# Attention heads placed between projection chunks, one sum of squares per half, and a reordered gate and merge stage, in a two-layer decoder trunk

## The chip, the cores and the metric

One Trainium2 chip, all 8 NeuronCores. Each core runs the same program on 2 of the 16 sequences, with no exchange between cores. The metric is the device time of one execution, in microseconds (us), taken on the slowest core.

## The reference, cut to what matters

The trunk has two layers. Width is 1024, the sequence 2048, the memory 256 tokens, with 4 heads of 256 in the cross-attention and 2816 hidden channels in the MLP.

```python
for l in range(DEPTH):                                    # DEPTH = 2
    h = rms_norm(x, mix_norm_g[l])
    proj = h @ w_in[l]
    a, gl, u_pool, g_conv, g_pool = jnp.split(proj, split_at, axis=-1)
    yc = a * sigmoid(gl)                                  # GLU, 512 channels
    yc = causal_dwconv(yc, conv_dw_w[l]) + conv_dw_b[l]   # 31 taps
    yc = silu(layer_norm(yc, conv_ln_g[l], conv_ln_b[l])) @ w_conv_out[l]
    zp = multiscale_pool(u_pool)
    yp = einsum("bsgc,gcd->bsgd", zp, w_pool_grp[l]).reshape(b, s, d) * pool_scale[l]
    merged = sigmoid(g_conv) * yc + sigmoid(g_pool) * yp
    x = x + merged @ w_out[l]
    hq = rms_norm(x, xattn_norm_g[l])                     # cross-attention into mem
    q = hq @ w_q[l];  k, v = split(mem_n @ w_kv[l])
    x = x + (softmax(q k^T / 16) v) @ w_o[l]              # 4 heads
    hf = rms_norm(x, ffn_norm_g[l])
    gate, val = split(causal_dwconv(hf @ w_up[l], ffn_dw_w[l]))
    x = x + (gelu(gate) * val) @ w_down[l]
return rms_norm(x, final_norm_g)
```

## The kernel before, in words

**Tiling.** Each core takes 2 sequences in 2 parts of T = 1024 positions (`hf` 0 and 1): 4 units, each through 2 layers, so **8 passes** of mixer, attention and MLP. Channels lie on the 128 partitions and positions on the free axis. The residual stream `X` is 8 tiles of 128x1024 float32, its normed copy `H` 8 tiles in bf16. Positions are worked in two halves of 512 (`s` = 0 and 1, `ST` = 512), because a matmul writes one PSUM bank of 128x512 float32. A *chunk* is 128 output channels of one half: 8 matmuls of 128x512 over the 8 input tiles (11 in the down projection) into one bank. An evacuation then reads the bank.

**What sets the order.** `Sched` keeps one list of instructions per engine, in the order in which the Python code adds them, and puts a semaphore wait where a tile written elsewhere is read, or a tile still in use is overwritten. There is no reordering: what is written first on an engine runs first there, and what stands behind a waiting instruction waits too. PSUM banks come from `Banks`, a rotation of 8: `P.next()` takes the bank used longest ago, so a chunk cannot start until that bank has been read. `P.take()` removes a bank from the rotation, and `P.release` appends it again. `defer(fn, lag)` puts work off until `lag` chunks later (`tick()` counts them).

**Weights** come in blocks of 1 MB through a ring of 5 slots (`ring_get`), issued on POOL. Copies between SBUF tiles and loads and stores of x are issued on SP.

**Mixer** (`mixer`). First `a` and `gl` are projected, half by half. `glu` takes the sigmoid of `gl` on ACT, and one DVE instruction multiplies the bank of `a` with it and writes the product in bf16 in *phase order* (position 4n+j goes to j*256+n), at line 763. After half 1, `to_phases` copies the product by DMA into the 16 convolution tiles `CV`. The convolution is 16 groups of 9 matmuls with 128x256, with the pooling branch, three up chunks and the first gate half-chunks between them. `stats_mm` sums for the LayerNorm. `ln_finish` computes mean and reciprocal deviation, then for each quarter q two DVE instructions on 128x1024 (line 865: subtract, multiply), four SILU activations of 128x256 and their copies by DMA (line 872). Then `gate_half` is called for the next gates. A gate k (0 to 15) is two half-chunks q = 2k and 2k+1, each with a sigmoid from its bank into a tile `GB`. There are 8 such tiles, so gate 8 needs the tile of gate 0, which the merge must have read. Before the merge, gates 0 to 7 are done. The merge goes over 8 output tiles i: for each half 5 matmuls from the silu and pooling results with the weights `WX`, and three DVE instructions (line 943, one at line 411, one at line 401) into `MG[i]`. Two gates follow i = 0, and one gate follows each of i = 1 to 6. In the last layer before a new sequence, and once at the start, the norm of the memory (`mem_squares`, `mem_finish`) lies in the same place.

**Output projections** (`residual_stage`) take the input tiles `MG`, the attention result `ATT`, or the MLP's hidden tiles. Two banks are taken for the sums of squares. All 8 chunks of half 0 come first (the first three, or two, as a *lead group* with the input tile as the outer loop), then the 8 of half 1. The evacuation of chunk `oc` is: DVE adds the bank to `X`, ACT squares, and DVE adds the square to the running sum of its group of four chunks:

```python
if oc % 4:
    TT("dve", sq.v(), sq.v(), prev_sq[s].v(), ALU.add)
prev_sq[s] = sq
if oc % 4 == 3:
    defer(lambda: MM(pn[s].v(), ONESK.v(), sq.v(), oc == 3, oc == 7), 3, tag)
```

So there are two matmuls with the ones matrix `ONESK` per half, three chunks after oc = 3 and after oc = 7. After the second come Ln and Exp on ACT (`norm_stats_fin`) and 8 instructions on DVE that write `H` (`norm_apply`, line 411), two per chunk. The half-0 ones stand between the evacuations of half 1.

**Attention** (`attn`). All 16 query chunks come first, half 0 and then half 1. Then for each head and half: 4 matmuls for the scores, 2 Exp on ACT, 2 matmuls with ones (the denominator), Ln and Exp on ACT, 4 matmuls with the values, 2 multiplications on DVE into `ATT`. The names in the trace are `AR,KV` for scores and values and `AR,ONES` for the denominator. Then the output projection.

**MLP** (`ffn`). It is not changed, apart from its down projection's use of `residual_stage`. In the last layer that stage also carries the final norm, the stores of the result, and the norm of the next unit's first input (`unit_norm`).

In the profile most instructions carry the line of a helper: L424 is every matmul, L397 every activation, L401 `tensor_tensor`, L411 `scalar_tensor_tensor`. `AR` is the arena in which most tiles lie. Tile names there tell operations apart.

## Time and profile before

| what | us |
|---|---|
| median of 3 runs | 4116.72 |
| lowest and highest | 4114.6, 4533.86 |
| the profiled execution | 4116.1 |
| its span, slowest core (core 6) | 4114.6 |
| spans of the 8 cores | 4102.6 to 4114.6 |
| PE busy | 3876.9 (94%) |
| DVE busy | 2683.5 (65%) |
| ACT busy | 1953.7 (47%) |

The profiled execution's time lies 1.5 us over its span and 0.6 us under the median, so terms worked out inside the span can be taken off the median as they are. The 8 passes lie one behind the other in the span, each a little over 500 us long. A busy PE is not PE at its peak: matmuls are pipelined, and their ends are modelled. What a stretch of matmuls lost is found by comparing its start-to-start time with the number of matmuls in it.

### The profile page before, as it was taken

The numbers are of one execution on the slowest core, as the hardware profiler recorded it, in microseconds if no ns is written. First come the engines' busy times: TensorE is split into PE (matmuls) and PEld (weight loads), VectorE is DVE, ScalarE is ACT, GpSimd is POOL, SyncE is SP. The second block draws the span as 40 slices with busy tenths as digits, with TensorE's granted clock in tenths as the row PEclk, the third lists the DMA queues.
The fourth block names the chain that finished last, engine by engine and source line by source line (L and its number), as shares of the span: only waits on it lengthen the run. The fifth ranks groups of instructions, "written<-read, shape, count | busy, mean of one in ns | idle before, by whom it ended". The sixth has DMA issues, their size and how long they took to land.

```text
span 4114.6 us, 56669 instructions; the slowest of 8 cores (4102.6 to 4114.6 us)
## 1 busy us (share of the span) xinstructions
PE 3876.9 (94%) x18224; PEld 1784.1 (43%) x18224; DVE 2683.5 (65%) x3336; ACT 1953.7 (47%) x3779; POOL 197.7 (5%) x379
## 2 busy tenths in 40 slices
PE   6999999999998999999989999999999999999998
PEld 3444444444443445434444444543444434444343
DVE  4538775387754876649675387653867549665587
ACT  3445444464444544446443464434644346452544
POOL 1000000000000000000010000000000000000000
PEclk9999999999999999999999999999999999999999
DMA  6443352434842345323464424534346424352342
GB/s 138 117 82 68 65 107 58 82 68 80 168 103 51 59 78 110 62 49 67 106 136 103 84 56 81 99 64 84 65 108 136 103 49 73 68 106 52 57 75 70
DMA packets 108815, 348.19 MB, mean 85 GB/s; under 512 B 11888, under 2 KB 46960, under 8 KB 83952
## 3 DMA queue, kind: packets, MB, share of 16 engines
q0 software_dynamic: 41760, 275.11, 37.0%
q1 hardware_dynamic: 66768, 69.46, 5.7%
q8 instruction: 155, 2.54, 0.3%
q14 instruction: 132, 1.08, 0.1%
HBM read 586.05 MB, written 16.78 MB: 147 GB/s over the span
## 4 chain that ended last, share of the span: by engine, by line
PE 81%; ACT 7%; DVE 6%; issue 3%; DMA 2%; SPq 0%; DVEq 0%; ACTq 0%; POOLq 0%; POOL 0%
PE ps L424 81%; DVE X L401 2%; ACT SQ L397 2%; DVE H L411 2%; ACT F L397 2%; ACT AR L397 2%; DMA AR<-AR 1%; DVE SQ L401 1%; DVE X L411 1%; ACT RS L397 0%; DMA AR<-xT 0%; SPq L872 0%; ACT L397 0%; DVE F L411 0%; DMA RING<-wst 0%
## 5 line engine op out<-in xcount | busy, mean ns | idle before, releaser
L424 PE MATMUL ps<-H,RING 128*128 128x512 bf16 x10240 | 2265.0, 381 | 66.4 <-ACT GB L397 25.3
L424 PEld LDWEIGHTS ps<-H,RING 128*128 128x128 bf16 x10240 | 1004.2, 98 | 1286.6 <-issue 110.7
L424 PE MATMUL ps<-AR,RING 128*128 128x512 bf16 x4864 | 1096.7, 386 | 0.0
L397 ACT ACTIVATE AR<-ps 128x512 bf16<-128x512 f32 (+1 forms) x1024 | 598.5, 600 | 637.8 <-PE ps L424 610.8
L411 DVE SCALAR_TENSOR_TENSOR F<-AR,VEC,F 128x1024 f32<-128x1024 bf16 (+1 forms) x576 | 687.9, 1194 | 111.8 <-ACT F L397 69.1
L424 PEld LDWEIGHTS ps<-AR,RING 128*128 128x128 bf16 x4864 | 482.7, 99 | 590.2 <-issue 39.1
L397 ACT ACTIVATE SQ<-X 128x512 bf16<-128x512 f32 x384 | 240.2, 629 | 599.8 <-DVE X L401 561.9
L401 DVE TENSOR_TENSOR X<-ps,X 128x512 f32<-128x512 f32 x512 | 339.6, 684 | 200.3 <-PE ps L424 200.2
L397 ACT ACTIVATE GB<-ps 128x512 bf16<-128x512 f32 x320 | 183.1, 604 | 433.1 <-PE ps L424 431.5
L397 ACT ACTIVATE GB<-F 128x1024 bf16<-128x1024 f32 x192 | 189.3, 986 | 287.0 <-DVE F L411 286.4
L515 POOL DMA_DIRECT2D RING<-wst x280 | 147.8, 528 | 3598.7 <-PE ps L424 3578.4
L401 DVE TENSOR_TENSOR SQ<-SQ 128x512 bf16<-128x512 bf16 x288 | 122.5, 425 | 258.6 <-ACT SQ L397 249.7
L401 DVE TENSOR_TENSOR AR<-ps,F 128x512 bf16<-128x512 f32 x128 | 82.4, 686 | 318.9 <-PE ps L424 305.0
L411 DVE SCALAR_TENSOR_TENSOR H<-X,VEC,RS 128x512 bf16<-128x512 f32 x320 | 222.3, 749 | 86.5 <-ACT RS L397 86.5
L397 ACT ACTIVATE F<-ps,VEC 128x512 f32<-128x512 f32 x352 | 242.9, 690 | 0.0
L411 DVE SCALAR_TENSOR_TENSOR GB<-AR,VEC,F 128x1024 bf16<-128x1024 bf16 x192 | 229.4, 1195 | 20.4 <-DVE F L411 0.5
L943 DVE TENSOR_TENSOR F<-ps,GB 128x512 f32<-128x512 f32 x128 | 88.0, 687 | 160.8 <-PE ps L424 160.7
L763 DVE TENSOR_TENSOR AR<-ps,GB 128x512 bf16<-128x512 f32 x64 | 154.9, 2446 | 34.9 <-ACT GB L397 21.5
L424 PE MATMUL ps<-AR,WX 128*128 128x512 bf16 x640 | 149.9, 379 | 3.8 <-DMA AR<-AR 3.4
L401 DVE TENSOR_TENSOR AR<-GB 128x1024 bf16<-128x1024 bf16 x192 | 124.3, 648 | 20.8 <-ACT F L397 0.9
L406 DVE TENSOR_SCALAR F<-AR,VEC 128x1024 f32<-128x1024 bf16 x192 | 135.0, 703 | 1.2 <-ACT AR L397 0.2
L424 PE MATMUL ps<-AR,KV 128*128 128x512 bf16 x512 | 122.1, 378 | 0.0
(75 smaller groups left out, 1954.5 us busy)
## 6 DMA issues: line engine op xcount, KB each, us to landing
RING<-wst POOLq DMA_DIRECT2D x184, 1024.0 KB, 9.3
RING<-wst POOLq DMA_DIRECT2D x64, 704.0 KB, 7.8
RING<-wst POOLq DMA_DIRECT2D x32, 768.0 KB, 6.7
AR<-AR SPq DMA_DIRECT2D x256, 64.0 KB, 3.5
X<-xT SPq DMA_DIRECT2D x64, 256.0 KB, 12.8
yT<-X SPq DMA_DIRECT2D x64, 256.0 KB, 9.4
AR<-xT SPq DMA_DIRECT2D x40, 256.0 KB, 7.0
WX<-wst POOLq DMA_DIRECT2D x8, 1280.0 KB, 15.9
```

The costliest lines, as they stand in the source:

```text
L397: S.add("act", lambda h: h.activation(out=out.ap, in_=in_.ap, func=func, scale=s, **kw), reads=rd, writes=out.keys)
L401: S.add(eng, lambda h: h.tensor_tensor(out=out.ap, in0=a.ap, in1=b.ap, op=op), reads=a.keys + b.keys, writes=out.keys)
L406: S.add(eng, lambda h: h.tensor_scalar(out=out.ap, in0=a.ap, scalar1=s, scalar2=None, op0=op0), reads=a.keys + k, writes=out.keys)
L411: S.add(eng, lambda h: h.scalar_tensor_tensor(out=out.ap, in0=a.ap, scalar=s, in1=b.ap, op0=op0, op1=op1), reads=a.keys + b.keys + k, writ ...
L424: S.add("pe", lambda h: h.matmul(out.ap, lhsT=lhsT.ap, rhs=rhs.ap, start=start, stop=stop), reads=lhsT.keys + rhs.keys, writes=out.keys)
L515: S.add("pool", lambda h, d=dst, s_=src: h.dma_start(out=d, in_=s_), reads=after, writes=RING[slot].v().keys, dma_sem="ring%d" % slot)
L763: S.add("dve", lambda h: h.tensor_tensor(out=o_ap, in0=a_ap, in1=g_ap, op=ALU.mult), reads=psa[c].v().keys + sub(sgs[c], s).keys, writes=G ...
L943: S.add("dve", lambda h, p_ap=p_ap, g_ap=g_ap, o_ap=o_ap: h.tensor_tensor(out=o_ap, in0=p_ap, in1=g_ap, op=ALU.mult), reads=psc.v().keys + ...
```

## The change

- **Sums of squares.** The running sum goes over all 8 chunks of a half and is added one chunk late: at chunk oc >= 2 DVE adds the squares of oc-2 and before to that of oc-1. At oc = 7 there is one more add. One matmul with `ONESK` per half is left, three chunks after oc = 7.
- **Attention.** Scores and heads of half 0 stand between the query chunks of half 1, and those of half 1 between the output chunks of half 0. `run_items` is the chunk loop taken out of `proj_group`.
- **Gates.** Half-gates 6 to 9 are computed inside `ln_finish`, one behind each quarter's four silus, and evacuated there as plain copies (Copy) to the float32 tiles F0 and F1. Their sigmoids are taken from there after gate 6. Gates 8, 9 and 10 get tiles of their own (`SQ`, `TW[0]`) and are computed before the merge. In the merge one gate follows each of i = 0 to 4.
- **LayerNorm.** The subtraction of quarter 1 stands before the multiplication of quarter 0.
- **GLU.** The multiplication walks its elements in another order: the output runs contiguously, and the two inputs are read with a step of 4 elements.

```diff
-            prev_sq = {}
+            sqs = [[], []]
...
                     ACT(sq.v(), sub(X[oc], s), AF.Square)
-                    if oc % 4:
-                        TT("dve", sq.v(), sq.v(), prev_sq[s].v(), ALU.add)
-                    prev_sq[s] = sq
+                    sqs[s].append(sq)
+
+                    def add():
+                        a, b_ = sqs[s].pop(0), sqs[s][0]
+                        TT("dve", b_.v(), b_.v(), a.v(), ALU.add)
+
+                    if oc >= 2:
+                        add()
                     tag = 2 if last else s
-                    if oc % 4 == 3:
-                        defer(lambda: MM(pn[s].v(), ONESK.v(), sq.v(), oc == 3, oc == 7), 3, tag)
                     if oc == 7:
+                        add()
+                        defer(lambda: MM(pn[s].v(), ONESK.v(), sq.v(), True, True), 3, tag)
...
-                    o_ap = GLU[c].ap.rearrange("p (j n) -> p n j", j=4)[:, s * 128:(s + 1) * 128, :]
-                    a_ap = psa[c].ap.rearrange("p (n j) -> p n j", j=4)
-                    g_ap = sub(sgs[c], s).ap.rearrange("p (n j) -> p n j", j=4)
+                    o_ap = GLU[c].ap.rearrange("p (j n) -> p j n", j=4)[:, :, s * 128:(s + 1) * 128]
+                    a_ap = psa[c].ap.rearrange("p (n j) -> p j n", j=4)
+                    g_ap = sub(sgs[c], s).ap.rearrange("p (n j) -> p j n", j=4)
...
+                for q in range(4):
+                    if q != 1:
+                        ln_op(q, mu, ALU.subtract)
+                    if q == 0:
+                        ln_op(1, mu, ALU.subtract)
+                    ln_op(q, va, ALU.mult)
                     for r in range(4):
...
-            def gate_half(q):
+                    gate_half(6 + q, GP[q])
+                    done.add(6 + q)
+
+            GP = [F[0].v(0, ST), F[0].v(ST, T), F[1].v(0, ST), F[1].v(ST, T)]
...
-                ACT(sub(gates[k], s), ps.v(), AF.Sigmoid)
+                if park is None:
+                    ACT(gates[k][s], ps.v(), AF.Sigmoid)
+                else:
+                    ACT(park, ps.v(), AF.Copy)
+                    parked.append((gates[k][s], park))
...
-            for k in range(3, 8):
+            for k in range(3, 11):
                 do_gate(k)
-                if has_mem and k == 6:
-                    mem_squares()
+                if k == 6:
+                    for o_, i_ in parked:
+                        ACT(o_, i_, AF.Sigmoid)
+                    if has_mem:
+                        mem_squares()
...
-                for _ in range(2 if i == 0 else 1):
-                    if k_next < 16:
-                        do_gate(k_next)
-                        k_next += 1
+                if k_next < 16:
+                    do_gate(k_next)
+                    k_next += 1
...
+            flush_tag((0,))
+            run_items(qi, 0)
+            flush()
+            for hd in range(3):
+                scores(hd, 0)
+                if hd == 0:
+                    lead_group(qi[0:4], 1)
+                else:
+                    run_items(qi[2 * hd + 2:2 * hd + 4], 1)
+                heads(hd, 0)
+            scores(3, 0)
+            scores(0, 1)
+            heads(3, 0)
+            heads(0, 1)
             wab = [ring_get(l, "woa0"), ring_get(l, "woa1")]
-            residual_stage([(wab[oc // 4], 512, (oc % 4) * 128, ATT) for oc in range(8)], "H", LB + 72, 3)
+            oi = residual_items([(wab[oc // 4], 512, (oc % 4) * 128, ATT) for oc in range(8)], "H", LB + 72)
+            for hd in range(1, 4):
+                scores(hd, 1)
+                run_items(oi[2 * hd - 2:2 * hd], 0)
+                heads(hd, 1)
+            run_items(oi[6:8], 0)
+            run_items(oi, 1)
```

The order of the instructions moves at three places. First PE, from the last matmuls of the LayerNorm sums (`SQ,MASK`) through the merge (`AR,WX`) into the output projection (`AR,RING`) of the first pass, before:

```order
L424 MATMUL ps<-SQ,MASK 128x512 x2
L424 MATMUL ps<-H,RING 128x512 x80
L424 MATMUL ps<-MEMN,ONESK 128x256 x8
L424 MATMUL ps<-AR,WX 128x512 x10
L424 MATMUL ps<-H,RING 128x512 x32
L424 MATMUL ps<-AR,WX 128x512 x10
L424 MATMUL ps<-H,RING 128x512 x16
L424 MATMUL ps<-AR,WX 128x512 x10
```

And the same place in the changed kernel; the last three rows are the end of the merge:

```order
L424 MATMUL ps<-SQ,MASK 128x512 x2
L424 MATMUL ps<-H,RING 128x512 x128
L424 MATMUL ps<-MEMN,ONESK 128x256 x8
L424 MATMUL ps<-AR,WX 128x512 x10
L424 MATMUL ps<-H,RING 128x512 x16
L424 MATMUL ps<-AR,WX 128x512 x10
...
L424 MATMUL ps<-H,RING 128x512 x16
L424 MATMUL ps<-AR,WX 128x512 x30
L424 MATMUL ps<-AR,RING 128x512 x80
```

48 matmuls of three gates moved ahead of the merge, and its last 30 matmuls (i = 5, 6 and 7) now stand together, with no gate between them and the output projection.

Second ACT, at the same place: the Ln and Exp of the LayerNorm (`RS<-RS`), the silus (`AR<-AR,VEC`) and the gates, before:

```order
L397 ACTIVATE RS<-RS 128x256
L397 ACTIVATE AR<-AR,VEC 128x256 x16
L397 ACTIVATE GB<-ps 128x512 x8
L397 ACTIVATE MEMN<-F 128x256 x8
L397 ACTIVATE GB<-ps 128x512 x2
```

And in the changed kernel:

```order
L397 ACTIVATE RS<-RS 128x256
L397 ACTIVATE AR<-AR,VEC 128x256 x4
L397 ACTIVATE F<-ps 128x512
L397 ACTIVATE AR<-AR,VEC 128x256 x4
L397 ACTIVATE F<-ps 128x512
L397 ACTIVATE AR<-AR,VEC 128x256 x4
L397 ACTIVATE F<-ps 128x512
L397 ACTIVATE AR<-AR,VEC 128x256 x4
L397 ACTIVATE F<-ps 128x512
L397 ACTIVATE GB<-ps 128x512 x4
L397 ACTIVATE GB<-F 128x512 x4
L397 ACTIVATE MEMN<-F 128x256 x8
```

The four copies `F<-ps` free four banks between the silus, and the four sigmoids `GB<-F` are new work behind them.

Third PE in the attention, from the queries (`H,RING`) into the output projection, before:

```order
L424 MATMUL ps<-H,RING 128x512 x128
L424 MATMUL ps<-AR,KV 128x512 x4
L424 MATMUL ps<-AR,ONES 128x512 x2
L424 MATMUL ps<-AR,KV 128x512 x8
L424 MATMUL ps<-AR,ONES 128x512 x2
...
L424 MATMUL ps<-AR,KV 128x512 x4
L424 MATMUL ps<-AR,RING 128x512 x48
L424 MATMUL ps<-SQ,ONESK 128x512
L424 MATMUL ps<-AR,RING 128x512 x32
L424 MATMUL ps<-SQ,ONESK 128x512
```

And in the changed kernel, the first head and then the place where the halves meet:

```order
L424 MATMUL ps<-H,RING 128x512 x64
L424 MATMUL ps<-AR,KV 128x512 x4
L424 MATMUL ps<-H,RING 128x512 x32
L424 MATMUL ps<-AR,ONES 128x512 x2
...
L424 MATMUL ps<-AR,ONES 128x512 x2
L424 MATMUL ps<-AR,KV 128x512 x12
L424 MATMUL ps<-AR,ONES 128x512 x2
L424 MATMUL ps<-AR,KV 128x512 x4
L424 MATMUL ps<-AR,ONES 128x512 x2
L424 MATMUL ps<-AR,KV 128x512 x8
L424 MATMUL ps<-AR,RING 128x512 x16
```

Between the scores of a head and its matmuls with ones there are now 16 or 32 matmuls of a projection, or, in the middle, 4 of another head.

## Rows read from the trace of the kernel before

**Rows 1.** Page, part 1: busy us, share of the span, instructions

```profile
PE 3876.9 (94%) x18224; PEld 1784.1 (43%) x18224; DVE 2683.5 (65%) x3336; ACT 1953.7 (47%) x3779; POOL 197.7 (5%) x379
```

**Rows 2.** Waits of PE: releaser, us in total, times, longest us

```profile
PE ps L424 <- DVE SQ L401: 85.0, 48, 4.3
PE ps L424 <- ACT AR L397: 31.6, 65, 0.5
```

**Rows 3.** Timeline of PE in the attention: start, us, work, [idle before <-releaser]

```profile
1779.13 1.03 PE L424 MATMUL ps<-AR,KV 128*128 128x512 bf16 x4
...
1786.73 0.76 PE L424 MATMUL ps<-AR,ONES 128*128 128x512 bf16 x2 [0.51 <-ACT AR L397]
...
1789.72 0.76 PE L424 MATMUL ps<-AR,ONES 128*128 128x512 bf16 x2 [0.51 <-ACT AR L397]
```

**Rows 4.** Timeline of PE in the attention's output projection

```profile
1803.17 10.52 PE L424 MATMUL ps<-AR,RING 128*128 128x512 bf16 x48
...
1831.64 0.59 PE L424 MATMUL ps<-SQ,ONESK 128*128 128x512 bf16 x1 [2.52 <-DVE SQ L401]
...
1836.83 3.62 PE L424 MATMUL ps<-H,RING 128*128 128x512 bf16 x16
```

**Rows 5.** Timeline of DVE in that projection, half 1

```profile
1824.92 1.42 DVE L411 SCALAR_TENSOR_TENSOR H<-X,VEC,RS 128x512 bf16<-128x512 f32 x2 [0.87 <-ACT RS L397]
...
1827.83 0.42 DVE L401 TENSOR_TENSOR SQ<-SQ 128x512 bf16<-128x512 bf16 x1 [0.89 <-ACT SQ L397]
1828.17 1.41 DVE L411 SCALAR_TENSOR_TENSOR H<-X,VEC,RS 128x512 bf16<-128x512 f32 x2
```

**Rows 6.** Timeline of PE, gates before the merge, and the merge

```profile
1646.61 13.98 PE L424 MATMUL ps<-H,RING 128*128 128x512 bf16 x64
1664.07 5.29 PE L424 MATMUL ps<-H,RING 128*128 128x512 bf16 x16 [3.48 <-ACT GB L397]
...
1687.67 3.62 PE L424 MATMUL ps<-H,RING 128*128 128x512 bf16 x16
1691.12 2.32 PE L424 MATMUL ps<-AR,WX 128*128 128x512 bf16 x10
```

**Rows 7.** Windows: us, busy us (x) of PE, PEld, DVE, ACT, POOL; PEclk; DMA share, GB/s

```profile
1664.00:1673.00 9.00, 8.65 (x35) 3.71 (x36) 0.23 (x1) 8.42 (x19) 0.53 (x1) 0.81 0.35 71
```

**Rows 8.** Timeline of ACT at the silus

```profile
1653.34 8.19 ACT L397 ACTIVATE AR<-AR,VEC 128x256 bf16<-128x256 f32 x16
1661.54 1.28 ACT L397 ACT_TABLE_LOAD   x1
1662.84 4.03 ACT L397 ACTIVATE GB<-ps 128x512 bf16<-128x512 f32 x8
```

**Rows 9.** Timeline of DVE in the merge

```profile
1692.26 0.69 DVE L943 TENSOR_TENSOR F<-ps,GB 128x512 f32<-128x512 f32 x1 [1.41 <-PE ps L424]
...
1694.32 0.68 DVE L943 TENSOR_TENSOR F<-ps,GB 128x512 f32<-128x512 f32 x1
```

**Rows 10.** Timeline of PE in the mixer's output projection

```profile
1715.73 10.52 PE L424 MATMUL ps<-AR,RING 128*128 128x512 bf16 x48
...
1745.63 0.38 PE L424 MATMUL ps<-SQ,ONESK 128*128 128x512 bf16 x1 [3.95 <-DVE SQ L401]
...
1750.98 3.62 PE L424 MATMUL ps<-H,RING 128*128 128x512 bf16 x16
```

**Rows 11.** Timeline of DVE in that projection, half 1, its first norm instructions

```profile
1738.90 1.41 DVE L411 SCALAR_TENSOR_TENSOR H<-X,VEC,RS 128x512 bf16<-128x512 f32 x2 [2.30 <-ACT RS L397]
```

**Rows 12.** Timeline of PE where a new unit begins

```profile
2109.71 3.40 PE L424 MATMUL ps<-H,RING 128*128 128x512 bf16 x15 [3.35 <-DVE AR L763]
2118.48 2.08 PE L424 MATMUL ps<-AR,GB 128*128 128x256 bf16 x9 [5.38 <-DMA AR<-AR]
```

**Rows 13.** Lines 763 and 943: count, ns min/median/max, first and last start

```profile
L763 DVE TENSOR_TENSOR AR<-ps,GB x64: 2410/2432/2683, 49.3 to 3641.0; 128x512 bf16<-128x512 f32 x64
L943 DVE TENSOR_TENSOR F<-ps,GB x128: 680/685/693, 149.0 to 3747.8; 128x512 f32<-128x512 f32 x128
```

More of the change, by code:

```diff
@@ L649, in proj_group, with run_items @@
                     lead_group(items[:lead[s]], s)
[L650 to L657 removed]
+                run_items(items[lead[s]:], s)
+        def run_items(items, s):
+            for blk, ncol, col0, rhs, evac in items:
+                b_ = blk(s) if callable(blk) else blk
+                nk = len(rhs)
+                ps = P.next()
+                for kc in range(nk):
+                    MM(ps.v(), b_.v(kc * ncol + col0, kc * ncol + col0 + 128), sub(rhs[kc], s), kc == 0, kc == nk - 1)
+                evac(s, ps)
+                tick()
         def norm_stats_fin(s, pn):
@@ L859, in ln_finish, with ln_op @@
                 P.release(pst)
-                for q in range(4):
+                def ln_op(q, vv, op):
                     y = YCQ[q]
                     y_ap = y.ap.rearrange("p (g n) -> p g n", g=4)
-                    for vv, op in ((mu, ALU.subtract), (va, ALU.mult)):
-                        v_ap = vv.ap.unsqueeze(1).to_broadcast([128, 4, 256])
-                        S.add("dve", lambda h, v_ap=v_ap, y_ap=y_ap, op=op: h.tensor_tensor(out=y_ap, in0=y_ap, in1=v_ap, op=op),
-                              reads=y.v().keys + vv.keys, writes=y.v().keys)
+                    v_ap = vv.ap.unsqueeze(1).to_broadcast([128, 4, 256])
+                    S.add("dve", lambda h: h.tensor_tensor(out=y_ap, in0=y_ap, in1=v_ap, op=op),
+                          reads=y.v().keys + vv.keys, writes=y.v().keys)
+                for q in range(4):
[4 more added lines that the diff above has]
+                    ln_op(q, va, ALU.mult)
                     for r in range(4):
@@ L881, in gate_half @@
                 if s == 0:
-                    gates[k] = GBR.next()
+                    if k in (8, 9):
+                        gates[k] = [SQB[2 * k - 16].v(), SQB[2 * k - 15].v()]
+                    else:
+                        gb = TW[0] if k == 10 else GBR.next()
+                        gates[k] = [sub(gb, 0), sub(gb, 1)]
                 col = half * 256 + ii * 128
@@ L1003, in attn, with scores @@
-            wab = [ring_get(l, "woa0"), ring_get(l, "woa1")]
-            residual_stage([(wab[oc // 4], 512, (oc % 4) * 128, ATT) for oc in range(8)], "H", LB + 72, 3)
+            qi = [(wqb[qc // 4], 512, (qc % 4) * 128, H,
+                   (lambda s, ps, qc=qc: ACT(sub(Q[qc], s), ps.v(), AF.Identity, scale=1.0 / 16))) for qc in range(8)]
+            expd = {}
+            def scores(hd, s):
+                expd[hd, s] = []
+                for mc in range(2):
+                    ps = P.next()
+                    for dc in range(2):
+                        MM(ps.v(), KT[2 * hd + dc].v(mc * 128, (mc + 1) * 128), sub(Q[2 * hd + dc], s), dc == 0, dc == 1)
+                    e = EBR.next()
+                    ACT(e.v(), ps.v(), AF.Exp)
+                    expd[hd, s].append(e)
@@ new lines, in heads @@
+            def heads(hd, s):
+                E = expd.pop((hd, s))
+                psd = P.next()
+                for mc in range(2):
+                    MM(psd.v(), ONES1.v(), E[mc].v(), mc == 0, mc == 1)
+                rd = F[(2 * hd + s) % 4]
+                ACT(rd.v(0, ST), psd.v(), AF.Ln)
+                ACT(rd.v(0, ST), rd.v(0, ST), AF.Exp, scale=-1.0)
+                for dc in range(2):
+                    pso = P.next()
+                    for mc in range(2):
+                        MM(pso.v(), VV[mc].v(hd * 256 + dc * 128, hd * 256 + (dc + 1) * 128), E[mc].v(), mc == 0, mc == 1)
+                    TT("dve", sub(ATT[2 * hd + dc], s), pso.v(), rd.v(0, ST), ALU.mult)
```

50 lines of the change are left out of this document (11 added, 39 removed).

## The prediction

> **What bounds the kernel now.** I read the page's busy times first. PE is busy for 94% of the span, DVE for 65% and ACT for 47% [rows 1], so only what PE waits for counts. The second view is PE's waits by releaser: the longest sum belongs to the matmuls with `ONESK`, 85.0 us in 48 waits for DVE's running sum of squares, and 31.6 us go to the attention's exponentials [rows 2]. The third is PE's timeline, because those sums miss what a wait leaves behind. I compare each stretch's length with its matmuls: 16 of 128x512 take 1691.12 - 1687.67 = 3.45 us when nothing disturbs them, so 0.2157 us each [rows 6]. Whatever a stretch takes above that is lost. All terms are of one pass near the middle of the span and are multiplied by 8. They come off the profiled execution's 4116.1 us, which is the median (4116.72) within 0.6 us.
>
> **Heads between projection chunks.** From the first scores (1779.13) to the first matmul of the output projection (1803.17) lie 24.0 us [rows 3, 4] for 80 matmuls, worth 17.3 us: 6.8 us lost. The rows show how: one head and half takes 1789.72 - 1786.73 = 2.99 us for 10 matmuls (2.16 us), because PE has nothing to do between the scores and the matmuls with ones. Now 16 or 32 projection matmuls (3.5 or 6.9 us) lie there. ACT does 4 activations of about 0.6 us per head plus 2 evacuations, 3.6 us, while PE does 26 matmuls, 5.6 us, so ACT stays ahead. In the middle only 4 matmuls of another head (0.86 us) cover two Exp (1.1 us): I leave 0.8 us there. Gain 6.0 a pass, 48 us. Bounds: 0 (ACT's queue holds the projection's banks for as long) and 54.
>
> **Attention's output projection, with one sum per half.** It takes 1836.83 - 1803.17 = 33.7 us [rows 4] for 131 matmuls (28.3 us): 5.4 us lost, 2.52 of it in one wait. DVE is in order there: add into X, wait for ACT's square (0.89), add the square, and in half 1 two norm instructions: 3.25 us per chunk [rows 5], where PE needs 1.73. With the add one chunk late the 0.89 goes, 2.36 us are left. The early sum (oc = 3), on which PE stood, is gone with its two matmuls (0.43 us). What is late next is the last sum. Count from the start of half 1: the sum of half 0 can go after two chunks (3.5); then come DVE's add, the square, Ln and Exp, about 2.8, so the norm instructions start at 6.3; four periods of 2.36 end at 15.8; two more chunks, a square and the last add take 2.8: 18.6. PE, with 8 chunks, a sum and the next stage's two chunks behind it, is there at 17.5. So about 1.0 us is left. Gain 5.4 + 0.4 - 1.0 = 4.8 a pass, 38 us. Bounds: 0.4 (the wait only moves) and 5.8.
>
> **Gates between the silus.** PE does 64 gate matmuls and then stands 3.48 us for a bank [rows 6], because ACT is in 16 silus (8.19 us) and a table load (1.28) and empties none [rows 8]. The 16 matmuls behind it take 5.29 us instead of 3.62, in a stretch whose mean granted clock is 0.81, so partly at 1.2 GHz instead of 2.4 [rows 6, 7]. Together 5.15 us. A copy after each four silus (2.05 us) now frees a bank every 2.6 us or so. Half-gate 14, the first to reuse a bank, comes 8 x 1.73 = 13.8 us after half-gate 6, long after the first copy. The four copies and the four late sigmoids cost ACT 8 x 0.5 to 0.6 us, in a stretch that is now 48 matmuls (10.4 us) longer. These also cover the silus' transfers, for which the merge sometimes waited. Gain 5.0 a pass, 40 us. Bounds: 5.2 above; below, see the table rival.
>
> By the Trainium skill (ScalarE: Activation LUTs, section on table sets) cheap functions such as copy are in every set, so these copies need no load. No row here shows a Copy behind a silu.
>
> **The end of the merge pays for the gates.** DVE takes 1694.32 - 1692.26 = 2.06 us per tile and half [rows 9], PE 5 matmuls, 1.08 us. A gate (3.45 us) behind each tile hid this. Tiles 5, 6 and 7 now have none. DVE starts 1692.26 - 1691.12 = 1.14 us after PE [rows 6, 9]. The output projection opens with three chunks side by side, and by the rotation the third needs the bank that DVE reads at the fifth of these six steps: 1.14 + 4 x 2.06 + 0.69 = 10.1 us, and a signal. PE has finished its 30 matmuls at 6.5 and can do 2 more: 3.3 us idle, and as after the 3.48 us above some matmuls at the lower clock, 1.3. So +4.6 a pass. Bounds 0 and 5.5. Queued behind: the whole projection.
>
> **Mixer's output projection.** 1750.98 - 1715.73 = 35.3 us [rows 10] for the same 131 matmuls: 7.0 us lost, 3.95 in one wait. It differs from the attention's by a table load before Ln: DVE waits 2.30 us there instead of 0.87 [rows 11, 5]. That load stays, so by the count above the last sum is ready 1.4 us later, at 20.0 against PE's 17.5: 2.4 us, and 0.6 for the clock. So 7.0 + 0.4 - 3.0 = 4.4 gained, and 4.6 paid to the merge: -0.2 a pass, -2 us. This is where most of an expected gain should vanish.
>
> **Down projection.** Of the 85.0 us of waits for the sum, 8.5 a pass (1.0 + 3.95 and 1.0 + 2.5) are in the other two stages, which leaves 17. Its chunks are 11 matmuls (2.37 us), as long as DVE's new 2.36, so nearly all goes: 14 us.
>
> **GLU.** It takes 2432 ns for 512 elements, with writes 512 bytes apart. The merge's multiplication reads its bank 512 bytes apart and writes contiguously in 685 ns [rows 13]. So I take 0.69 us for the new form, whose reads step by 4 elements. Bounds: 0.68, and 4.9 (each of the two stepped reads as slow as the stepped write). In most passes no PE wait hangs on it. Where a new unit begins (3 times) PE stands 3.35 us for a bank that GLU holds and 5.38 for the transfer issued behind it [rows 12]; the other two show less of the second. I take 3.35, 1.4 of clock and 1.5 of the transfer, since the DMA queue is full there: 6.3 x 3 = 19 us.
>
> The Trainium skill has a rule against this part: by Advanced Engine Details and Errata, section Memory Cachelines, PSUM has lines of 8 bytes, and pairs of elements should be contiguous; it speaks of matmuls. The new read steps 16 bytes. By that rule GLU would stay slow, which is the third rival. The row of line 943 (685 ns) speaks against it, and the slow writes (2432 ns) fit its rule for SBUF.
>
> **Sum.** 48 + 38 + 40 - 2 + 14 + 19 = 157 us. 4116.7 - 157 = **3960 us**.
>
> **Rivals.**
> 1. *The queues of ACT and DVE bound the mixed stages.* The ATT multiplications, adds and squares now share an in-order queue with evacuations, so PE waits for banks in the middle of chunks. For it: DVE's period in half 1 exceeds PE's chunk already [rows 5]. Against it: ACT is 47% busy. Half of the heads' and the projection's gain goes: 3960 + 24 + 19 = 4003.
> 2. *Copy is not in silu's table set*: 8 loads of 1.28 us [rows 8] a pass, 10.3 us on ACT. The gates' 5 us is lost and another 5.3 spent at the merge's start: 3960 + 82 = 4042.
> 3. *GLU's stepped reads cost what the stepped writes did*: only the units' starts are lost, 3960 + 19 = 3979.
> 4. *The other side: both stepped reads are slow*, 4.9 us. The a/gl stage (27.6 us of matmuls) holds 8 x 2.4 = 19.5 us of GLU already, and with the norm and tap instructions DVE has little room, so 8 x 2.45 = 19.6 us a pass end up on PE: 3960 + 157 + 19 = 4136, slower than before. It decides from 2.43 + (157 - 19)/64 = 4.6 us. Line 943's row speaks against it.
>
> **How the numbers follow.** Forecast 0.68; rivals 1 to 4: 0.18, 0.03, 0.07, 0.04. Low end: if the new waits (0.8, 1.0, 4.6 and 3.0 a pass) were about 60% smaller, 45 us less, 3915. High end: rival 1 with 17 us more, 4020; beyond lie rivals 2 and 4 and a tail. A measurement of this kernel can tell about 2% (82 us) from no change; 4034 is that border. Faster by over 2%: 0.92; within 2%: 0.07 (rivals 2 and 4, the tail of 1); slower by over 2%: 0.01.
>
> **What would show it.** Right: PE's waits for `AR,ONES` near 5 us instead of 34; waits for the sum of squares near 25 us, all at the last sum of a half; no wait of PE for ACT's `GB` tiles behind the silus; a new gap of some 3 us between the last `AR,WX` and the first `AR,RING`, released by DVE; GLU at 0.69 us. Wrong: table loads between the silus; GLU above 2 us; matmul groups in the attention far over 0.2157 us each. If the merge's gap is missing, the time comes out near 3925.

## The result and the profile after

The changed kernel ran in 3961.56, 3947.66 and 3949.14 us. The ratio to the kernel before is **0.9604, interval 0.956 to 0.9649**: 4.0% faster, where 3960 us (0.962) was forecast. Most kernels also had executions some ten to some hundred microseconds longer, in which the cores of one die showed a lower clock; the ratios and times given here are of the other executions. Where two chips are compared I add the *middle core*: the median core span of the die that was the faster one in a run, and of these the median over all runs (before: 4111 us on the first experiments' chip, 4124 on the second, 4114 on the third; changed kernel: 3929).

That the total fits does not mean that its parts do. So I read the profile after in the same order as the one of before. The page gives the execution (core 2, the slowest) and its busy times:

```profile
span 3960.0 us, 56824 instructions; the slowest of 8 cores (3921.7 to 3960.0 us)
PE 3809.3 (96%) x18176; PEld 1776.8 (45%) x18176; DVE 2580.8 (65%) x3384; ACT 1955.8 (49%) x3811; POOL 206.6 (5%) x379
```

PE's matmuls went from 18224 to 18176: the 48 early sums of squares. DVE's busy time fell by 103 us and ACT's stayed as it was [rows 1]; ACT's share rose from 47% to 49% only because the span is shorter. PE's waits by releaser (us in total, times, longest us):

```profile
PE ps L424 <- DMA AR<-AR: 33.8, 6, 12.5
PE ps L424 <- DVE SQ L401: 27.8, 17, 2.5
PE ps L424 <- DVE F L976: 21.8, 18, 1.5
```

Three things are to be seen. The sum of squares has 27.8 us left of 85.0, and the attention's exponentials, 31.6 us before, are not in the list [rows 2]. DVE's `F L976` is new: it is the merge's multiplication, line 943 before. And the longest is now a transfer, `AR<-AR`, the copies of the GLU's product into the convolution's tiles. It was forecast to shrink. In the profile of before it read

```profile
PE ps L424 <- DMA AR<-AR: 12.6, 7, 5.4
```

**The merge's end** (PE's timeline; start, us, work, [idle before <-releaser]):

```profile
1170.33 6.64 PE L424 MATMUL ps<-AR,WX 128*128 128x512 bf16 x30
1178.47 0.38 PE L424 MATMUL ps<-AR,RING 128*128 128x512 bf16 x1 [1.50 <-DVE F L976]
1179.13 0.38 PE L424 MATMUL ps<-AR,RING 128*128 128x512 bf16 x1 [0.28 <-DVE F L411]
1180.52 1.87 PE L424 MATMUL ps<-AR,RING 128*128 128x512 bf16 x4 [1.02 <-DVE F L976]
...
1211.12 0.38 PE L424 MATMUL ps<-H,RING 128*128 128x512 bf16 x1 [0.15 <-DVE H L411]
1211.78 2.10 PE L424 MATMUL ps<-H,RING 128*128 128x512 bf16 x9 [0.29 <-DVE H L411]
1215.62 0.38 PE L424 MATMUL ps<-SQ,ONESK 128*128 128x512 bf16 x1 [1.74 <-DVE SQ L401]
```

From 1170.33 to 1180.52 are 10.19 us for 32 matmuls (6.90): 3.29 us lost, the new gap. The three rows behind it are the end of the mixer's output projection: 10 matmuls (2.16) between 1211.12 and 1215.62, so 2.3 us lost to norm instructions and the last sum of squares, 2.6 with the stretch just before. In the attention the middle, where the cover was thinnest, and the end of its output projection read:

```profile
1249.94 2.12 PE L424 MATMUL ps<-AR,KV 128*128 128x512 bf16 x8
1252.06 3.61 PE L424 MATMUL ps<-AR,RING 128*128 128x512 bf16 x16
...
1285.51 3.62 PE L424 MATMUL ps<-H,RING 128*128 128x512 bf16 x16
1290.19 0.38 PE L424 MATMUL ps<-SQ,ONESK 128*128 128x512 bf16 x1 [1.06 <-DVE SQ L401]
```

8 matmuls (1.73 us) take 2.12: 0.4 us is lost there, the same in all eight passes, and nowhere else among the heads. The last sum costs 1.2 us (4.68 for 16 matmuls).

**ACT at the silus** has one evacuation behind each four, and a table load at either end only:

```profile
1118.09 1.28 ACT L397 ACT_TABLE_LOAD   x1 [1.47 <-DVE AR L875]
1119.38 2.08 ACT L397 ACTIVATE AR<-AR,VEC 128x256 bf16<-128x256 f32 x4
1121.37 0.57 ACT L397 ACTIVATE F<-ps 128x512 f32<-128x512 f32 x1
...
1129.30 1.28 ACT L397 ACT_TABLE_LOAD   x1
```

**DVE.** The GLU's 64 instructions (ns min/median/max), and from DVE's timeline the first norm instructions in the mixer's output projection:

```profile
L773 DVE TENSOR_TENSOR AR<-ps,GB x64: 679/691/693, 49.6 to 3502.3; 128x512 bf16<-128x512 f32 x64
```

```profile
1203.45 1.41 DVE L411 SCALAR_TENSOR_TENSOR H<-X,VEC,RS 128x512 bf16<-128x512 f32 x2 [3.55 <-ACT RS L397]
...
1205.71 1.41 DVE L411 SCALAR_TENSOR_TENSOR H<-X,VEC,RS 128x512 bf16<-128x512 f32 x2
```

GLU fell from 2432 to 691 ns. DVE's period in half 1 is 1205.71 - 1203.45 = 2.26 us.

**Where a unit begins**, PE's timeline and the queue of SP on the same core; below it SP's queue of before, at the same place:

```profile
1030.70 27.79 PE L424 MATMUL ps<-H,RING 128*128 128x512 bf16 x128
1070.99 2.08 PE L424 MATMUL ps<-AR,GB 128*128 128x256 bf16 x9 [12.50 <-DMA AR<-AR]
```

```profile
1023.22 27.86 SPq L674 DMA_DIRECT2D yT<-X  x14
1051.22 3.33 SPq L758 DMA_DIRECT2D AR<-AR  x4
1054.64 7.54 SPq L674 DMA_DIRECT2D yT<-X  x2
1062.27 11.84 SPq L758 DMA_DIRECT2D AR<-AR  x12
```

```profile
1066.60 31.42 SPq L671 DMA_DIRECT2D yT<-X  x14
1099.00 3.26 SPq L748 DMA_DIRECT2D AR<-AR  x4
1102.35 1.01 SPq L671 DMA_DIRECT2D yT<-X  x2
1103.79 8.38 SPq L748 DMA_DIRECT2D AR<-AR  x8
```

The wait for the GLU's bank is gone and the 128 matmuls of `a` and `gl` run through in 27.8 us. But the transfer is waited for 12.50 us instead of the 5.38 and less of before [rows 12]. The windows say why (us; busy of PE, PEld, DVE, ACT, POOL; PEclk; DMA share; GB/s), of after and then of before:

```profile
1020.00:1070.00 50.00, 38.28 (x175) 16.87 (x174) 33.20 (x52) 15.51 (x26) 5.27 (x8) 0.91 1.02 192
```

```profile
1060.00:1110.00 50.00, 42.47 (x183) 17.81 (x181) 44.98 (x53) 16.79 (x28) 4.54 (x7) 0.97 0.98 190
```

The core's 16 DMA engines are busy throughout in both kernels, moving 190 GB/s: stores of the old unit, loads of the new one's x, weights. The copies stand behind 14 and 2 stores of 256 KB in SP's queue: the 14th store lands at 1070.5 us, the first copy at 1070.7. In PE's timeline of before, the convolution starts at this place with

```profile
1111.57 2.08 PE L424 MATMUL ps<-AR,GB 128*128 128x256 bf16 x9 [2.63 <-DMA AR<-AR]
```

The wait is now 9.9 us longer, for two reasons. PE comes to the convolution 35.3 us after the first store, where it was 42.3 (3.4 of these 7 us are the bank wait that is gone). And the copies are there 47.8 us after the first store, where it was 45.0 us. From issue to landing the stores take, by the page's median,

```profile
yT<-X SPq DMA_DIRECT2D x64, 256.0 KB, 19.4
```

and 9.4 before. The wait differs between cores and sets their spans. PE's sums for `AR<-AR` on cores 0 to 7 are 19.5, 2.4, 33.8, 21.6, 23.5, 13.2, 27.1 and 9.2 us (mean 18.8; before 7.4 to 12.8, mean 10.1), and the spans of the two cores that wait least and most are 3921.7 us (core 1) and 3960.0 us (core 2).

**Stage by stage.** I took the start of the first matmul of each stage in both timelines (the convolution's, the merge's, the first scores, the MLP's) and subtracted the lengths, over 8 passes. From the convolution to the end of the attention, 141.0 us went; forecast for that block, without the attention's last sum, which falls behind its border, 124 + 8 = 132. From the MLP to the next convolution, with the down projection and the start of the next unit, 12.5 us went; forecast 33 - 8 = 25. Ahead of the first convolution 1.1 went. The block in which the heads and gates lie gave 9 more than forecast, the block with the transfers gave half. In that block the three stretches that end at a new unit's convolution, called *the three starts* below, took 837.9 us on the slowest core before and 833.8 after: 4 us gained there. On the mean of the eight cores it was 837.2 and 821.7, so 15.5.

### The profile page after: what moved, and what is told of

Read it like the earlier page. It is cut to its first block, busy times and chain, and to the rows that moved or that the text cites. A ratio compares the mean times of both kernels' runs of the same rounds, so it can differ in the third digit from the quotient of the medians.

```text
span 3960.0 us, 56824 instructions; the slowest of 8 cores (3921.7 to 3960.0 us)
## 1 busy us (share of the span) xinstructions
PE 3809.3 (96%) x18176; PEld 1776.8 (45%) x18176; DVE 2580.8 (65%) x3384; ACT 1955.8 (49%) x3811; POOL 206.6 (5%) x379
## 4 chain that ended last, share of the span: by engine, by line
PE 89%; DVE 4%; DMA 3%; issue 2%; ACT 2%; SPq 1%; DVEq 0%; ACTq 0%; POOLq 0%; POOL 0%
PE ps L424 89%; DMA AR<-AR 2%; DVE X L401 1%; DVE F L411 1%; DVE F L976 1%; DVE SQ L401 1%; ACT AR L397 1%; DVE H L411 0%; DMA AR<-xT 0%; ACT F L397 0%; SPq L674 0%; DVE X L411 0%; DMA RING<-wst 0%; ACT SQ L397 0%; SPq L889 0%
## 5 line engine op out<-in xcount | busy, mean ns | idle before, releaser
L424 PE MATMUL ps<-AR,RING 128*128 128x512 bf16 x4864 | 1074.7, 381 | 22.5 <-DVE F L976 20.2
L397 ACT ACTIVATE AR<-ps 128x512 bf16<-128x512 f32 (+1 forms) x1040 | 607.6, 600 | 633.2 <-PE ps L424 606.1
L397 ACT ACTIVATE GB<-F 128x1024 bf16<-128x1024 f32 (+1 forms) x224 | 206.9, 938 | 288.9 <-DVE F L411 288.1
L397 ACT ACTIVATE GB<-ps 128x512 bf16<-128x512 f32 x240 | 139.1, 599 | 337.0 <-PE ps L424 335.5
L401 DVE TENSOR_TENSOR SQ<-SQ 128x512 bf16<-128x512 bf16 x336 | 140.3, 418 | 30.1 <-ACT SQ L397 25.9
L976 DVE TENSOR_TENSOR F<-ps,GB 128x512 f32<-128x512 f32 x96 | 65.8, 686 | 134.8 <-PE ps L424 134.8
L397 ACT ACTIVATE SQ<-ps,VEC 128x256 bf16<-128x256 f32 x256 | 107.5, 472 | 49.0 <-PE ps L424 45.4
```

The lines of the kernel that those rows point to most:

```text
L397: S.add("act", lambda h: h.activation(out=out.ap, in_=in_.ap, func=func, scale=s, **kw), reads=rd, writes=out.keys)
L401: S.add(eng, lambda h: h.tensor_tensor(out=out.ap, in0=a.ap, in1=b.ap, op=op), reads=a.keys + b.keys, writes=out.keys)
L424: S.add("pe", lambda h: h.matmul(out.ap, lhsT=lhsT.ap, rhs=rhs.ap, start=start, stop=stop), reads=lhsT.keys + rhs.keys, writes=out.keys)
L976: S.add("dve", lambda h, p_ap=p_ap, g_ap=g_ap, o_ap=o_ap: h.tensor_tensor(out=o_ap, in0=p_ap, in1=g_ap, op=ALU.mult), reads=psc.v().keys + ...
```

## The experiments

Four kernels ran on each of three chips, each kernel beside runs of the kernel before on its own chip. Differences against the changed kernel are differences of ratios times 4117 us. The changed kernel's own interval is 0.9%, so each of them is uncertain by about 20 us; what the profile of a run shows at the place in question is therefore read beside it: the waits, and the lengths of these same stages, mean of the eight cores. Each kernel has one profiled execution.

### Is the unit's start bound by the transfers?

**e1: the GLU in its old element order** (writes 512 bytes apart), the rest as changed.

```diff
-o_ap = GLU[c].ap.rearrange("p (j n) -> p j n", j=4)[:, :, s * 128:(s + 1) * 128]
-a_ap = psa[c].ap.rearrange("p (n j) -> p j n", j=4)
+o_ap = GLU[c].ap.rearrange("p (j n) -> p n j", j=4)[:, s * 128:(s + 1) * 128, :]
+a_ap = psa[c].ap.rearrange("p (j n) -> p n j", j=4)
```

(and the same for the sigmoid's tile)

> The changed kernel with the GLU multiplication in its old element order (2.43 us instead of 0.69), all else kept. Theory A (the transfers bound the start of a unit): the first convolution group waits there for 4 MB of stores of the result that were issued ahead of its copies, so a slower GLU changes only who is waited for: within 5 us of the changed kernel's 3955. Theory B (my forecast's step): the faster GLU is worth 19 us at the three starts of a unit, so about 3974. Both: the five other passes show no difference.

**e2: the changed kernel, the 16 stores of a finished unit issued behind the 16 copies.** `norm_apply` only keeps them, and the mixer issues them after its `flush_all()`:

```diff
+                if (b, hf) == units[-1]:
+                    store()
+                else:
+                    pend_out.append(store)
...
                 flush_all()
+                while pend_out:
+                    pend_out.pop(0)()
```

> The changed kernel with the 16 stores of a unit's result issued on SP behind the 16 copies into the convolution tiles, at the three places where another unit follows. Theory A (the copies stand behind the stores in SP's queue and in the DMA engines): PE's waits for AR<-AR, 33.8 us in the profile, fall to under 5, and with the lower clock after them some 30 to 37 us go: 3918 to 3925. Theory B (the DMA engines are full anyway, with weights and the next input, so order does not matter): the waits stay above 25 us and the time stays within 8 us of 3955.

Measured: e1 0.963 (0.9608 to 0.9652), so 11 us slower than the changed kernel (23 by the middle core, 3952 for 3929); e2 0.9548 (0.953 to 0.9566), 23 us faster than it, where 30 to 37 were expected. The two ran on one chip, and the 34 us between them have an interval of 12 either way. PE's waits of e1 and of e2 (slowest core each):

```profile
PE ps L424 <- DMA AR<-AR: 25.6, 8, 9.7
PE ps L424 <- DVE AR L773: 10.1, 3, 3.4
```

```profile
PE ps L424 <- DMA AR<-AR: 1.3, 2, 0.8
```

In e1 the bank wait of before is back, 3.4 us at each of three starts, and so is a long transfer wait, mean 16.7 us over the cores. The long transfer wait is not the new GLU's doing: it is there without it. What the GLU is worth here the times leave open, 11 or 23 us; the three starts took 833.9 us for the changed kernel's 821.7, so 12.2. In e2 the transfer wait is gone, on every core at most 4.5 us, the spans lie within 3921.4 to 3936.9, and the three starts took 803.3 us. e2's windows and PE's timeline:

```profile
1020.00:1070.00 50.00, 49.49 (x233) 22.48 (x232) 38.51 (x61) 22.19 (x37) 5.30 (x9) 1.00 0.78 143
```

```profile
1038.93 27.79 PE L424 MATMUL ps<-H,RING 128*128 128x512 bf16 x128
1066.55 1.15 PE L424 MATMUL ps<-AR,GB 128*128 128x256 bf16 x9
```

The convolution follows without a gap, and the clock stays up. The stores issued ahead of the copies were the cause. Whether they hold the copies back by their place in the queue or by the load that they put on the DMA engines is not separated: e2 changes both, and in its window the share is 0.78 instead of 1.02. The Trainium skill (DMA: Bandwidth & Descriptors, section on queues, rings and completion order) says that descriptors on one DMA engine are consumed in ring order; the trace agrees as far as it goes, since the first copy lands just behind the 14 stores issued ahead of it.

**e8 and e9: the same two edits on the kernel before**, the new GLU order alone, and the late stores alone.

> The kernel before with the new element order of the GLU multiplication alone. Theory A (the start of a unit is bound by the DMA engines): the waits of PE for DVE AR L763 (10.1 us in three) go and its waits for AR<-AR there grow by nearly as much; 4110 to 4117. Theory B (the forecast's term): 19 us less, 4098. In the five other passes nothing changes although DVE is 14 us a pass less busy.

> The kernel before with the 16 stores of a unit's result issued behind the copies into the convolution tiles. Theory A (the same backlog was there before the change, hidden in part by PE's own delays): PE's waits for AR<-AR, 7.4 to 12.8 us by core, fall to the 2 or 3 us of the merge, but the 3.35 us waits for the GLU's bank stay: 8 to 12 us less, ratio 0.997. Rival (the change itself made the backlog, before it there was none to speak of): ratio 1.000.

Measured: e8 0.991 (0.9886 to 0.9934), 37 us with an interval of 10 either way, more than either theory gave; e9 0.9948 (0.9928 to 0.9968), 21 us, double what was expected. Both are likely too large: on these two chips one die's clock was 0.972 to 0.984 in the runs of before, where the first chip has 0.986. By the middle cores (median of the runs) e8 gains 36 us and e9 12; by the lowest of them, which are least touched by the clock, e8 gains 4107.2 - 4084.3 = 23 us and e9 4108.8 - 4099.9 = 9. The three starts, 837.2 us before, took 819.1 in e8 and 833.2 in e9: 18.1 and 4.0 less. In e8 the bank wait is gone and so is most of the transfer wait (at most 5.4 us by core, 7.4 to 12.8 before):

```profile
PE ps L424 <- DMA AR<-AR: 2.2, 3, 1.1
```

The copies are issued when half 1's GLU has run; a GLU that is 1.7 us shorter lets them start sooner, and the bank wait and the transfer wait both fall: 10.1 + 7.6 us on the mean core. So on the kernel before, the forecast's 19 us were there. In the changed kernel the starts show 12.2 of them (e1). That the other edits ate the rest, by bringing PE to a queue that was still full, is argued and not shown: e4 below does not touch the starts, and its 814.6 us for 821.7 says how far two profiled executions differ there.

**e10: both, late stores with the old GLU**, to see whether the GLU counts when the transfers no longer bind.

> Stores behind the copies, as in the second experiment, with the GLU's old element order. Theory A (once the transfers no longer bound the start of a unit, the GLU's time shows): 3 x 3.35 us for the bank, the clock behind it and the later copies: 12 to 20 us more than the second experiment's 3936, so 3948 to 3956. Theory B (GLU was worth the 10 us of the first experiment for other reasons, equal in both): 3946 with no wait of PE for DVE AR.

Measured 0.9558 (0.9515 to 0.96), against e2's 0.9548 on another chip. The bank wait is back:

```profile
PE ps L424 <- DVE AR L778: 10.1, 3, 3.4
PE ps L424 <- DMA AR<-AR: 2.6, 3, 1.1
```

The ratios do not settle it, since their intervals overlap; the middle cores do: 3943 against e2's 3923, and 3 of these 20 us lie between the chips. The three starts took 820.6 us, for e2's 803.3. With the transfers out of the way the GLU is worth some 17 us, near the 19.

### The parts of the gain

**e4: the attention in its old order**, all 16 query chunks, then head after head, then the output projection; one sum per half is kept. `heads` and `scores` are written back as one loop over `hd` and `s`, with `proj_group` ahead of it and `residual_stage` behind.

> The changed kernel with the attention in its old order (all queries, then all heads one behind the other, then the output projection), the one sum per half kept. Theory A (the heads' own waits are what the interleaving takes away, and nothing else): 8 x 6.4 = 51 us more, 4006, with PE's waits for AR,ONES back at 34 us and the output projection as in the changed kernel. Rival: the output projection also gained from the heads between its chunks (its first half has slack on DVE), then 60 us or more.

**e5: the old sums of squares**, the rest as changed.

```diff
-                    sqs[s].append(sq)
...
-                    if oc >= 2:
-                        add()
+                    if oc % 4:
+                        TT("dve", sq.v(), sq.v(), prev_sq[s].v(), ALU.add)
+                    prev_sq[s] = sq
+                    if oc % 4 == 3:
+                        defer(lambda: MM(pn[s].v(), ONESK.v(), sq.v(), oc == 3, oc == 7), 3, tag)
```

> The changed kernel with the old running sums: one sum per four chunks, added at once, two matmuls with ONESK per half. Theory A (the prediction's terms): mixer's projection 7.0 - 2.6 + 0.4 = 4.8 us a pass, attention's 5.4 - 1.2 + 0.4 - 1.0 (its first half now has slack between the heads) = 3.6, down projection 2.0: 10.4 x 8 = 83 us, 4038. Rival (the sums cost only what PE waited for them, 85 - 28 = 57 us, and the waits at the lower clock nothing): 4012. PE's waits for DVE SQ should be 70 to 85 us.

Measured: e4 0.973 (0.9703 to 0.9756), 52 us back for 48 forecast; e5 0.979 (0.9771 to 0.9809), 77 us back. The waits of e4, and of e5:

```profile
PE ps L424 <- ACT AR L397: 31.8, 65, 0.5
PE ps L424 <- DVE SQ L401: 27.9, 17, 2.5
```

```profile
PE ps L424 <- DVE SQ L401: 83.5, 44, 4.3
```

Each edit brings back its own wait, and not the other's. The two do not lean on each other: neither rival, in which the sums took what the heads gave, or the other way, holds. The middle cores agree for e4 (3977, 48 more than 3929), and for e5 (4022, 93 more, 80 if the chips' 13 us come off). From the convolution to the MLP e4 took 51.7 us more. In the forecast the sums had 38 + 14 and, in the mixer, (7.0 + 0.4 - 3.0) x 8 = 35: 87 in all, of which 77 were found. The rival in which the sums cost only their waits, 57 us, lies 20 lower, at the edge of the uncertainty; the middle core speaks against it.

**e6: no half-gates between the silus.**

```diff
-                    gate_half(6 + q, GP[q])
-                    done.add(6 + q)
```

> The changed kernel without the four half-gates between the silus: half-gates 6 to 9 come behind all sixteen silus with their sigmoids, everything else kept, gates 8 to 10 still ahead of the merge. Theory A: PE stands 3 to 3.5 us for a bank behind the silus again and loses 1.7 at the lower clock: 8 x 5.1 = 41 us, 3996. Rival (the 48 further matmuls ahead of the merge would have absorbed the wait, so that parking is worth nothing): within 8 us of 3955.

**e7: gates 8 to 10 back in the merge**, two behind i = 0, the half-gates between the silus kept.

```diff
-            for k in range(3, 11):
+            for k in range(3, 8):
...
-            k_next = 11
+            k_next = 8
```

> The changed kernel with gates 8 to 10 back in the merge (two gates behind i = 0, one behind each of 1 to 6), the four parked half-gates kept. Theory A (the gates ahead of the merge cover the silus' copies): the gap of 3.3 us between merge and projection goes (-26), but the merge now starts 17.3 us after the LayerNorm's sums, before the last silu's copy has landed, and PE waits about 4 us a pass for AR<-AR (+35): about 3964. Theory B (the copies were covered anyway): 3929.

Measured: e6 0.9664 (0.9626 to 0.9703), 25 us back, with some 24 us of uncertainty either way; 40 were forecast. Its middle core is 3972, 43 above the changed kernel's, 30 if the chips' 13 us come off. From the convolution to the MLP it took 33 us more. The wait it restores is the forecast's, at 2.6 us a pass instead of 3.2; before, then e6:

```profile
PE ps L424 <- ACT GB L397: 25.3, 8, 3.5
```

```profile
PE ps L424 <- ACT GB L397: 21.0, 8, 2.9
```

For e7 there is no ratio with an interval. Its 4014.01 over the lowest of before on that chip (4149.4) is 0.967, about 29 us slower than the changed kernel, where 9 were expected (middle core 3979: 50, or 37 with the chips' difference; from the convolution to the MLP 48). Its waits and the merge's start in one pass:

```profile
PE ps L424 <- DMA AR<-AR: 65.9, 16, 7.6
```

```profile
640.42 0.38 PE L424 MATMUL ps<-AR,WX 128*128 128x512 bf16 x1 [1.40 <-DMA AR<-AR]
647.99 2.99 PE L424 MATMUL ps<-AR,WX 128*128 128x512 bf16 x7 [7.20 <-DMA AR<-AR]
```

`F L976` is not in its list at all, so the gap at the merge's end did come from the gates put forward. But the merge now stands 7.20 us for the silus' copies, and some 7 us in each of six passes of eight; in the two with the norm of the memory PE waits 5 us for ACT instead (10.3 us on `MEMN`). The silus with the evacuations between them take 1129.30 - 1119.38 = 9.9 us instead of 8.2 [rows 8], and the 48 matmuls (10.4 us) that covered their transfers are gone. The three gates in front are what pays for the half-gates; they cost 3.3 us a pass at one end and save more at the other.

### The gap at the merge's end

**e3: the merge's gates behind i = 2 to 6** instead of 0 to 4.

```diff
-                if k_next < 16:
+                if i >= 2 and k_next < 16:
```

> The changed kernel with the five gates of the merge behind tiles i = 2 to 6 instead of 0 to 4, so that only i = 7 has no gate behind it, as before the change. Theory A (the gap between merge and output projection is DVE's lag over three tiles without gates): the waits of PE for F L976 and F L411 (21.8 and 2.3 us) vanish, DVE's lag after the first three tiles is made up behind the gates, and 8 x 3.3 = 26 us go: 3929. Theory B (the lag only moves to the front of the merge, where PE then waits for banks): within 8 us of 3955.

Measured 0.9562 (0.9535 to 0.9589), 17 us faster than the changed kernel. PE's waits:

```profile
PE ps L424 <- DVE F L976: 5.3, 6, 2.2
```

The gap at the merge's end is gone in all eight passes. In the two that hold the norm of the memory, 2.5 to 2.9 us of waits for DVE stand inside the merge instead; those are the 5.3 us. From the merge to the first scores 21 us went, so the 26 expected, 8 x 3.3, less these 5.

### Do the two gains add, and is there more?

**e11: e2 and e3 together.**

> The changed kernel with both: the merge's gates behind i = 2 to 6, and the stores behind the copies. If the two are independent, the gains add: 3955 - 20 - 17 = 3918, ratio 0.951. If the wait taken away in the merge only reappears at the start of a unit or in the projection's last sum, 3930.

**e12: e11, and in the mixer's output projection the last sum, Ln, Exp and the norm instructions of half 1 come 5 chunks later instead of 3.**

```diff
+                        lg = 5 if s == 1 and lead == 3 else 3
-                        defer(lambda: MM(pn[s].v(), ONESK.v(), sq.v(), True, True), 3, tag)
-                        defer(lambda: norm_stats_fin(s, pn), 3, tag)
+                        defer(lambda: MM(pn[s].v(), ONESK.v(), sq.v(), True, True), lg, tag)
+                        defer(lambda: norm_stats_fin(s, pn), lg, tag)
```

(`norm_apply` likewise. Only the mixer's projection passes a lead of 3; the attention's takes its items from `residual_items` without one and keeps its 3 chunks.)

> As the run before, and in the mixer's output projection the matmul with ONESK of half 1, with the norm behind it, five chunks late instead of three. Theory A (PE stands for the last sum only because the matmul comes too early; the norm of half 1 is needed six chunks later and has slack): the waits of 1.7 to 2.5 us in the mixer's projection go, 8 x 2 = 16 us less than the run before, 3902, ratio 0.948. Theory B (the norm of half 1 then comes too late for the queries of half 1): no gain or a few us lost, with PE waiting for DVE H.

Measured: e11 0.9468 (0.9443 to 0.9494), median 3913.38 us; e12 0.9445 (0.9399 to 0.9491), 3896.6. Expected of e11: 23 + 17 = 40 under the changed kernel's 0.9604, which makes 0.951; it came out a little better. In e12 the wait for the sum fell from e11's 27.9 to

```profile
PE ps L424 <- DVE SQ L401: 11.1, 9, 2.3
```

Those nine waits are the eight of the attention's projection, 1.1 to 1.3 us each, and the last of the kernel; the mixer's are all gone. From the merge to the first scores 22.8 us went, where 16 were expected. Five of e12's six runs (3893.55 to 3902.92, the sixth 3937.39) lie below all of e11's on the same chip (3907.82 to 3920.13), and its middle core is 3879 for 3901. The ratios' intervals overlap. e12 beats both kernels: 5.5% under the one before.

## Why the prediction was right, and where not

Terms as the prediction put them, with what the runs gave:

- **Heads, 48 us: right.** Undoing it costs 52, and PE has no wait for the exponentials. I left 0.8 us in the middle and 0.4 was lost. From the first scores to the MLP PE has no wait in any pass, so rival 1 falls: ACT and DVE held no bank that PE wanted there.
- **One sum per half, 38 + 14 + 35: right, 77 measured** for the three stages together. The count by which the last sum is late (1.0 and 2.4 us) gave 1.2 and 2.6. DVE's period was put at 2.36 and is 2.26. That a wait of 2.52 or 3.95 us becomes one of 1 to 2.5, and doesn't go, came from following DVE's queue to its end.
- **Gates between the silus, 40 us: right in kind, the size not settled.** No table load was added (80.8 us in 63 loads in both kernels), which is rival 2's end. It also agrees with the rule of the Trainium skill (ScalarE: Activation LUTs) that I had cited. e6 gives 25 by the ratio, 30 to 43 by the middle core and 33 by the stages; 40 is not excluded. That the gates ahead of the merge also cover the silus' transfers I had named without a price. e7 shows it: the cover is worth more than the gap that the moved gates cause.
- **The merge's gap, 3.3 us a pass idle: measured 3.29.** The clock behind it was put at 1.3 us in every pass. It fell in four passes of eight, where it cost 1.5 to 1.7, so 0.8 on average: 4 us too dear.
- **GLU, 0.69 us: right, 691 ns.** Rivals 3 and 4 fall: a read 16 bytes apart in PSUM and 8 apart in SBUF costs DVE no more than a contiguous one. The Trainium skill's rule on PSUM lines (Advanced Engine Details and Errata, Memory Cachelines) speaks of matmuls; for DVE's reads the measurement decides, and no penalty is seen.
- **Units' starts, 19 us: this step failed.** The sentence was "I take 3.35, 1.4 of clock and 1.5 of the transfer, since the DMA queue is full there". The bank's 3.35 did go, three times. The transfer's wait did not shrink by 1.5 at each start but grew, from a mean of 10.1 us per core to 18.8, and on the slowest core from 12.6 to 33.8. With the down projection's share in them, the three starts gained 4 us on the slowest core instead of 19. I had seen that the queue was full and drew the wrong conclusion. The copies land when the stores ahead of them are through. What PE saves between the first store and the copies is then waited for there, as the 7 us by which it comes sooner show. The heads do not lie between the two, and which edit brought PE forward beyond the bank's 3.35 no run isolates. As a term of its own the GLU was priced about right, 18.1 us at the starts on the kernel before and 17.3 with late stores; what failed is its sum with the rest. Late stores (e2) remove the wait, and give 23 us.

Against 157 us, the profiled executions differ by 4116.1 - 3961.6 = 154.5. That this fits to 3 us is partly luck. The block with the starts gave some 13 us too little, and the block of heads, sums and gates 9 too much: of these the heads' middle (0.4 a pass), the mixer's last sum (0.4) and the merge's clock (0.5) make 10. The range, 3915 to 4020, would have held each of these errors by itself.

## What to carry to other kernels

When a stretch has the DMA engines full, a gain inside it can show up as a longer wait at its end: look in the issuing queue for bulk stores that nobody waits for ahead of small copies that PE does wait for, and issue those stores later. A last sum that closes a stage stays late by DVE's whole backlog, so count its queue to the end rather than striking out the wait that you see. Gates or other free chunks are best laid where the slower engine is behind, at a merge's end, and as many of them as cover the transfers at its start.

## What the runs showed of the hardware

- **Step of a read and step of a write differ on DVE.** 512 elements with bf16 writes 512 bytes apart take 2432 ns; with float32 reads 16 bytes apart and bf16 reads 8 apart, and contiguous writes, 691 ns; the merge's multiplication, with float32 reads 512 bytes apart and contiguous writes, 680 to 693 ns [rows 13].
- **The same idle time does not always lower the clock.** The 3.48 us of before in one piece was followed by a granted clock of 0.81 [rows 7]. The merge's gap (1.50, 0.28 and 1.02 us, single matmuls between) was followed by a dip in four passes (the first row, mean clock 0.79 over 8 us) and none in four others (the second):

```profile
1178.00:1186.00 8.00, 6.23 (x21) 2.38 (x22) 5.58 (x9) 0.00 (x0) 0.00 (x0) 0.79 0.13 26
1654.00:1660.00 6.00, 4.65 (x21) 1.99 (x22) 5.16 (x8) 0.00 (x0) 0.00 (x0) 1.00 0.04 7
```

  What sets these passes apart was not found.
- **Eight cores with one program differ at a full DMA stretch**, from 2.4 to 33.8 us of waiting for the same copies. The slowest core sets the time: late stores took 23 us off the time and 23 off the slowest span of the profiled execution (3960.0 to 3936.9), 19 off the mean span of its eight cores (3944.2 to 3925.3), and 6 off the middle core (3929 to 3923).
